# A two-layer hybrid trunk on one core: both attention heads of a tile handled as a pair, and several steps placed elsewhere in their slots

## What is computed

```python
for i in range(DEPTH):                      # 2
    h = rmsnorm(x, norm_w[i])
    (u, s5_gate, z, xbc, dt_raw, q, k, v, att_gate, merge_logits) = split(h @ w_in[i])
    y_s5 = s5_mixer(u, ...) * silu(s5_gate)            # diagonal complex SSM, gelu, GLU
    y_ssd = ssd_mixer(z, xbc, dt_raw, ...)             # dt = softplus(dt_raw + bias); 16 heads of 64
    y_att = window_attention(q, k, v, att_gate, ...)   # 16 query heads, 4 key heads, width 64
    branches = einsum('blnw,nwd->blnd', stack(y_s5, y_ssd, y_att), w_branch[i])
    x = x + (sum_n sigmoid(merge_logits)[n] * branches[n]) @ w_out[i]

# ssd_mixer, inside a chunk and across chunks: y = (C B^T * exp(segsum(a))) @ (x * dt) + x * D
# window_attention: q, k = rope(rmsnorm(.)); s = q k^T / 8, masked to two chunks
#   m = max(max(s), sink); p = exp(s - m); o = (p / (sum(p) + exp(sink - m))) @ v
```

## Time and profile before

| | us |
|---|---|
| median of 3 runs | 1928.88 (1927.85 to 1931.57) |
| the profiled execution, its own time | 1926.38 |
| its span, first to last instruction | 1924.7 |
| PE busy | 1867.9 |
| DVE busy | 1387.2 |
| ACT busy | 959.2 |

### The profile page before, as it was taken

How to read it: one execution, slowest core, us unless ns; L and a number is a source line. 1 busy time by engine, 2 the same in 40 slices (tenths; PEclk the granted TensorE clock), 3 DMA queues, 4 the chain that set the end, 5 groups by cost and what they waited for, 6 DMA issues and landing times.

```text
span 1924.7 us, 35397 instructions
## 1 busy us (share of the span) xinstructions
PE 1867.9 (97%) x11720; PEld 1574.7 (82%) x11720; DVE 1387.2 (72%) x1945; ACT 959.2 (50%) x1144; POOL 538.2 (28%) x616
## 2 busy tenths in 40 slices
PE   6999999999999999999999999999999999999998
PEld 6888888777777788888889888887777778888887
DVE  6876666777776777666678766677776876776656
ACT  5334444656656555333444344456656565543344
POOL 5053444161442010002402433442442410100043
PEclk9999999999999999999999999999999999999999
DMA  7355555556455456665554555555555555566655
GB/s 284 139 191 189 191 189 190 178 190 207 162 193 177 151 200 256 232 229 209 205 183 169 172 184 189 196 199 197 172 174 183 174 191 178 197 243 238 234 198 203
DMA packets 80785, 376.98 MB, mean 196 GB/s; under 512 B 20848, under 2 KB 27536, under 8 KB 41872
## 3 DMA queue, kind: packets, MB, share of 16 engines
q1 hardware_dynamic: 76560, 360.00, 53.5%
q0 software_dynamic: 2368, 10.99, 1.6%
q10 hardware_dynamic: 1760, 4.75, 0.6%
HBM read 356.00 MB, written 21.79 MB: 196 GB/s over the span
## 4 chain that ended last, share of the span: by engine, by line
PE 71%; DVE 10%; issue 7%; POOL 5%; ACT 3%; DMA 2%; POOLq 0%; DVEq 0%; SPq 0%; ACTq 0%
PE mm L1708 21%; PE mm L1709 10%; PE mm L1739 10%; PE mm L1741 10%; PE mm L1740 10%; DVE w_lo L1036 2%; PE mm L1692 1%; PE mm L1693 1%; PE mm L1694 1%; DMA raw<-in_stream 1%; ACT w_hi L715 1%; POOL cl L567 1%; PE b L1851 1%; POOL tB L543 1%; POOL ssum L512 1%
## 5 line engine op out<-in xcount | busy, mean ns | idle before, releaser
L1036 DVE TENSOR_TENSOR w_lo<-raw,w_hi 128x2048 fp32r<-128x2048 f32 x299 | 696.8, 2331 | 194.5 <-ACT w_hi L715 179.8
L715 ACT ACTIVATE w_hi<-raw 128x2048 fp32r<-128x2048 f32 x299 | 571.3, 1912 | 471.2 <-DMA raw<-in_stream 469.1
L1708 PE MATMUL mm<-h_both,w_hi 128*128 128x512 f32 x1792 | 635.3, 399 | 0.3 <-DVE h_both L1627 0.3
L1709 PE MATMUL mm<-h_both,w_lo 128*128 128x256 f32 x1792 | 502.4, 280 | 0.0
L1708 PEld LDWEIGHTS mm<-h_both,w_hi 128*128 128x128 f32 x1792 | 336.6, 188 | 84.5 <-DVE h_both L1627 1.0
L1709 PEld LDWEIGHTS mm<-h_both,w_lo 128*128 128x128 f32 x1792 | 338.3, 189 | 0.1
L1739 PE MATMUL mm<-w_lo,h_both 128*128 128x512 f32 x768 | 316.7, 412 | 0.0
L1741 PE MATMUL mm<-w_hi,h_both 128*128 128x512 f32 x768 | 300.6, 391 | 0.0
L1740 PE MATMUL mm<-w_hi,h_both 128*128 128x512 f32 x768 | 300.1, 391 | 0.0
L696 POOL TENSOR_TENSOR ssum<-ssum,proj 128x256 f32<-128x256 f32 x32 | 77.2, 2412 | 379.0 <-ACT proj L1005 351.9
L1739 PEld LDWEIGHTS mm<-w_lo,h_both 128*128 128x128 f32 x768 | 144.1, 188 | 41.5 <-issue 12.1
(11 more groups left out here) (338 smaller groups left out, 2674.0 us busy)
## 6 DMA issues: line engine op xcount, KB each, us to landing
raw<-in_stream SPq DMA_DIRECT2D x300, 1024.0 KB, 4.8
gscr<-gt SPq DMA_DIRECT2D x48, 256.0 KB, 6.2
gin<-gscr SPq DMA_DIRECT2D x24, 512.0 KB, 5.7
bd<-in_bdense SPq DMA_DIRECT2D x16, 384.0 KB, 5.2
lam<-lscr SPq DMA_DIRECT2D x128, 32.0 KB, 3.4
crow<-cscr POOLq DMA_DIRECT2D x16, 256.0 KB, 5.4
x_old<-out POOLq DMA_DIRECT2D x2, 2048.0 KB, 10.7
out<-proj ACTq DMA_DIRECT2D x8, 512.0 KB, 5.3
```

Of the source, the lines that this page charges most:

```text
L715: e.activation(w_hi[:, j % RAW, :], raw[:, j % RAW, :], ACT.Copy).then_inc(hi_done, 1)
L1036: e.tensor_tensor(w_lo[:, j % RAW, :], raw[:, j % RAW, :], w_hi[:, j % RAW, :].bitcast(F32), ALU.subtract).then_inc(lo_done, 1)
L1708: e.matmul(mm[:, j % 2, :], w_hi[:, j % RAW, w], h_both[:, k].rearrange("p a t -> p (a t)"), start=k == 0, stop=False)
L1709: ins = e.matmul(mm[:, j % 2, 256:512], w_lo[:, j % RAW, w], h_hi[:, k, :], start=False, stop=k == KT - 1)
```

## The change

In the gate stage the two heads of a tile are handled together. `pr`, `small` and the scores get room for both heads; `stt` and `sc` go, since the products are made in place in `ex` and `pr`. `a1`, `ssd_y`, `a2` and `a3` each issue both heads' matmuls, alternating between heads, once per tile, with scores and transposes in b7 or b5 for head 0 and b6 for head 1. `a1` and `ssd_y` stand after t3, `a2` in the fourth quarter of t5, `a3` after t5. ScalarE's `att_exp`, `att_norm` and `pt_out` and most of VectorE's steps now stand ahead of `hi` and `lo` of their slot; `back`, `scan` and `forth` of the S5 mixer too. The GELU's square stays in step 9, its tanh goes to step 10 and its last product to step 11. The sinks are negated once on GpSimd (`cur2`).

In the slices `dt_t` goes from slice 3 to 4, `dt_s` from VectorE's slot 4 to 5, `dt` from slice 5 to 6, `dt_exp` from ScalarE's slot 5 to 7, `dt_softplus` from VectorE's slot 11 to 12, `cs` from slice 13 to 15, `k_rot` from 12 to 13, `gm` from VectorE's slot 14 to 13 and the keys' rotation from 13 to 14; ScalarE's `prep_end` from 14 to 15.

```diff
@@ ScalarE, gate stage
-                        def att_exp(h):
-                            W.wait(MV, f"nm{h}")
-                            W.wait(MA, f"pn1{h ^ 1}", 0 if h else 1)
+                        def att_exp():
+                            W.wait(MV, "es")
+                            for h in range(2):
+                                for b, (lo_c, hi_c) in enumerate(((0, 128), (128, 384))):
...
                         for t in range(6):
                             s = 6 * c + t
+                            if t == 4:
+                                att_exp()
+                                att_norm()
+                            if s % QUAD == QUAD - 1:
+                                gate(s // QUAD, 0)
+                            if t == 1:
+                                inv_sqrt(MA, "q", qh[:], rq[:], rv[:], lambda: W.wait(MV, "q_v"))
+                            if t == 5:
+                                pt_out(0)
+                                pt_out(1)
+                            if s % QUAD == QUAD - 1:
+                                gate(s // QUAD, 1)
+                            if t == 1:
+                                decay_exp()
+                            hi(nb, s + LEAD)
@@ VectorE, slices
-                    if n == 11:
+                    if n == 12:
                         dt_softplus()
@@ VectorE, gate stage
-                        def st_make(h):
-                            W.wait(MA, "ex")
-                            W.wait(MP, "ys0" if h else "ys1", 0 if h else 1)
-                            MV.mark(tt_(stt_[:], ex[:, h], flat(gm[:, bass.ds(I // 2, 1), :]), ALU.mult), f"ST{h}")
+                        def st_make():
+                            W.wait(MA, "ex")
+                            MV.mark(tt_(ex[:], ex[:], gm[:, bass.ds(I // 2, 1), :].broadcast_to([P, 2, 384]), ALU.mult), "ST")
...
+                            if t == 3:
+                                att_scores()
+                                lo(nb, s + LEAD)
...
+                            if t == 4:
+                                att_sum()
...
+                                MV.mark(e.scalar_tensor_tensor(xc[:], xc[:], cc[:, 27:28], ps_ssd, ALU.mult, ALU.add), "yv")
+                                lo(nb, s + LEAD)
@@ TensorE, slices
-                    if n == 13:
+                    if n == 15:
                         W.wait(LV, "dta")
@@ TensorE, gate stage
-                        def ssd_y(h):
-                            W.wait(MV, f"ST{h}")
-                            if not h:
-                                W.wait(MV, "yatt", 1)
-                            rows = slice(64 * h, 64 * h + 64)
-                            e.matmul(ps_ssd[rows, :], xdt[:, 0, h, :], stt_[:, 0:256], start=True, stop=False)
-                            MP.mark(e.matmul(ps_ssd[rows, 128:256], xdt[:, 1, h, :], stt_[:, 256:384], start=False, stop=True), f"ys{h}")
+                        def ssd_y():
+                            W.wait(MV, "ST")
+                            for h in range(2):
+                                e.matmul(ps_ssd[64 * h:64 * h + 64, :], xdt[:, 0, h, :], ex[:, h, 0:256], start=True, stop=False)
+                            for h in range(2):
+                                ins = e.matmul(ps_ssd[64 * h:64 * h + 64, 128:256], xdt[:, 1, h, :], ex[:, h, 256:384], start=False, stop=True)
+                            MP.mark(ins, "ys")
...
+                        def a1():
...
+                            for lo_c, hi_c, q in ((0, 128, 0), (128, 384, 1)):
+                                for h in range(2):
+                                    rows = slice(64 * h, 64 * h + 64)
+                                    ins = e.matmul((b7, b6)[h][:, lo_c:hi_c], qh[rows, q * P:q * P + P], kcur[rows, 0:hi_c - lo_c], start=True, stop=True)
+                            MP.mark(ins, "A1")
...
-                                if q == 2 and t == 4:
-                                    a1(1)
                                 if q == 3 and t == 5:
-                                    a2(1)
+                                    a2()
...
                             if t == 3:
-                                ssd_y(0)
-                                a1(0)
-                            if t == 4:
-                                a2(0)
-                                ssd_y(1)
+                                a1()
+                                ssd_y()
                             if t == 5:
-                                a3(0)
-                                a3(1)
+                                a3()
```

More of the change, by code:

```diff
@@ L878, in pt_out, with att_norm @@
+                        def att_norm():
+                            W.wait(MV, "rden")
+                            for h in range(2):
+                                for b, (lo_c, hi_c) in enumerate(((0, 128), (128, 384))):
+                                    q = 28 + 2 * b + h
+                                    MA.mark(e.activation(pr[:, h, lo_c:hi_c], pr[:, h, lo_c:hi_c], ACT.Copy, scale=small[:, q:q + 1]), f"pn{b}{h}")
                         def pt_out(h):
[L879 removed]
@@ L1469, in _, with att_sum @@
+                        def att_sum():
+                            W.wait(MA, "pes")
+                            MV.mark(tt_(small[:, 24:28], small[:, 20:24], small[:, 16:20], ALU.add), "den")
+                            W.wait(MV, "den")
+                            W.wait(MA, "pn11", 1)
+                            MV.mark(e.reciprocal(small[:, 28:32], small[:, 24:28]), "rden")
                         for t in range(6):
@@ L1909, in a1 @@
-                        def a1(h):
-                            W.wait(MV, f"sc{h ^ 1}", 0 if h else 1)
-                            if not h:
-                                W.wait(MV, "qh")
-                                if c == 0:
-                                    W.wait(MG, "vcur")
-                                    e.wait_ge(k_in, keys)
-                            rows = slice(64 * h, 64 * h + 64)
-                            e.matmul(b7[:, 0:128], qh[rows, 0:P], kcur[rows, 0:P], start=True, stop=True)
-                            MP.mark(e.matmul(b7[:, 128:384], qh[rows, P:TOK], kcur[rows, :], start=True, stop=True), f"A1_{h}")
@@ new lines, in a2, with a3 @@
+                        def a2():
+                            W.wait(MA, "pn11")
+                            for h in range(2):
+                                for q in range(3):
+                                    ins = e.transpose((b5, b6)[h][:, q * P:q * P + P], pr[:, h, q * P:q * P + P], C("ident"))
+                            MP.mark(ins, "A2")
+                        def a3():
+                            W.wait(MA, "pt1")
+                            W.wait(MV, "yv")
+                            for h in range(2):
+                                e.matmul(ps_att[64 * h:64 * h + 64, :], vcur[:, 0, :], pt[:, h, 0:256], start=True, stop=False)
+                            for h in range(2):
+                                ins = e.matmul(ps_att[64 * h:64 * h + 64, 128:256], vcur[:, 1, :], pt[:, h, 256:384], start=False, stop=True)
+                            MP.mark(ins, "A3")
```

208 lines of the change are left out of this document (88 added, 120 removed).

## The result

| | before | after |
|---|---|---|
| median of the runs, us | 1928.37 (1923.67 to 1931.57) | 1878.46 (1876.60 to 1878.89) |
| the profiled execution, its own time | 1926.38 | 1878.58 |
| its span | 1924.7 | 1876.9 |
| PE busy | 1867.9 | 1826.9 |

A forecast was written before the change was run, and what follows sets the result against it. TensorE was taken as the bound (PE busy 97%). Gains of 32.0 + 6.6 + 3.4 + 4.8 + 3.2 = 50.0 us took the profiled 1926.4 to 1876.4, plus 2.5 for the median: 1878.9 us, range 1871 to 1885.

The forecast's parts named there:

- The paired matmuls: Gate stage: two stops per tile go, `a2` grows, second heads cost next to nothing; 2.00 us per tile, 32.0 us gained.
- The wait for the SSD product: Gate stage: TensorE's six waits for `stt` go, as VectorE makes the product ahead of `lo`; 6.6 us gained.
- the remaining edits: S5 steps, GELU's spread and gates: moved within slots, cost nothing as long as VectorE and ScalarE have room.
- The third rival: Gate stage: ScalarE's two-head copy before `a3` and the second gate bring small waits, about 8 us: 1887 us; chance 0.10.
- The fourth rival: Gate stage, t5: `a2` waits for both heads' probabilities, 4.5 us per tile, kernel slower at about 1950 us; chance 0.04.
- The slices: Input slices, both layers: earlier `lam_T`, shorter waits for `dta` and regained clock, 3.4 + 4.8 + 3.2 us gained.
- For `dta`: Slices: of 8.8 us of waits 4.0 come back before slice 15, 4.8 gained, plus 3.2 of lost clock.
- For `rtok`: Slices: `dt_s` leaves VectorE's slot 4, so `lam_T` comes 1.7 us earlier in both layers; 3.4 us gained.
- The offset: Whole kernel: the median of the runs lies 2.5 us above the profiled execution, 1878.9 against 1876.4 us.
- The signs named in advance: Profile after: no t4 stop, `a2` about 0.66 us, `a1` paired, no `stt` or `dta` wait, turn some 5 us shorter.

The follow-up runs named there:

- x6: The changed kernel with the second head of `ssd_y` issued alone at half of t4, and `yv` behind `lo`: 1889.4 us.
- x7: x1 with `ssd_y` issued between the two heads of `a1`, so that these are no neighbours: 1882.5 us.
- x8: The changed kernel with VectorE's remainder put back ahead of the rotated queries and the SSD product in step t2: 1891.6 us.
- x1: The changed kernel with the two steps of the GELU's inner term on VectorE moved behind the sum of the exponentials: 1872.3 us.
- x2: The changed kernel with GpSimd's last three steps on `bw` done on one column instead of 256, output not the reference's: 1862.8 us.
- x9: x1 with the two tanh for the gates on ScalarE at the end of t2 instead of t4: 1871.4 us.

## Why the prediction was right, and where it was not

The forecast was 1878.9 us, the median is 1878.5. The mechanism held, but that the number came out so close is luck: its terms erred both ways by up to 9.6 us.

- **The paired matmuls, 32.0 us: right.** The stops of 1.05 and 1.33 us went, 37.8 us; `a2` grew by 0.33 us (forecast 0.32), 5.3 us; the second head of `a1` costs 0.01 us (forecast 0.06). That is 32.5 us. The argument from the earlier trace rows, four records in the time of two, held: x6 shows it for `ssd_y` and x7 for `a1`, each by taking the heads apart. The heads of `a3` stood side by side in every run.
- **The wait for the SSD product, 6.6 us: right.** The stop after t3 fell by 6.8 us over 16 tiles. x8 shows that VectorE's order can undo it; the share of TensorE's new order is open.
- **Not counted, and gained: 5.1 us.** `a2` had waited for `pt` (3.2 us over the price of its matmuls) and `q_rot` for the queries (1.9 us). Both were small waits of before that the sum passed over; they went with the same edits.
- **The step that failed: the remaining edits at nothing.** It reasoned from VectorE's busy share of the earlier trace rows that there is room. The room was there, but not in front of the sum of the exponentials: the stops for `a3` grew by 9.6 us (9.2 us in the list of waits). The third rival had the place and nearly the price (8 us), for the wrong reason. It charged ScalarE's second copy, in every tile; the runs show 1.3 to 1.8 us in six tiles, from the GELU's inner term (x1), GpSimd's hold on VectorE (x2) and ScalarE's order (x9). In x2 the second copy is still there and the wait is not. The fourth rival's chain was estimated at 8 us from scores to transposes; `a2` never waited for it, so its margin was real. That rival divided 54 us by 16 tiles where the sum has 50.0, which is 3.1 us per tile and not 3.4.
- **The slices, 11.4 us: too small, 16.4.** For `dta` the forecast was 4.8 + 3.2 = 8.0 us. The waits of VectorE's bank reads that took its place are 3.6 us in all: 1.0 and 1.4 us before slice 15, where 1.7 and 2.3 were forecast, and 0.9 and 0.3 us before slice 13, where none was. The clock stayed at 1.00 behind those before slice 15 (windows of after, below), so 5.2 + 3.2 = 8.4 us came. For `rtok` the forecast was 3.4 us. The waits of that stop fell from 7.6 to 3.8 us, and 4.0 us of low clock behind it (3.5 by the starts, 1.4 of them luck), which I had looked for only behind `dta`, went as well; `dt_t`, now at a stop of its own, took 1.1 us back, 0.7 of them a wait for the remainder before slice 4: 6.7 us. The rest, 1.3 us, is the start of the second layer's slices.

```profile
122.60:127.00 4.40, 4.35 (x36) 4.35 (x37) 4.40 (x9) 0.83 (x2) 2.71 (x2) 1.00 0.66 242
1044.10:1048.00 3.90, 3.84 (x32) 3.85 (x33) 3.90 (x9) 0.34 (x2) 2.51 (x1) 1.00 0.63 256
```

- **The other stages, nothing: 2.8 us lost.** Of these, 1.1 us is in the eight pairs behind the gate stage (46.0 to 46.5 us in each layer), and it is there in the experiments too. The remainder lies in stages that differ by 2 us from one run of this set to another. I did not look for its cause.
- **The offset: wrong, and it hid a loss.** The forecast put the median 2.5 us above the profiled execution, as before. After the change the two are 0.1 us apart, so the profiled execution is 2.2 us over its forecast of 1876.4. In numbers: 50.0 - 4.3 (gate stage) + 5.0 (slices) - 2.8 (others) = 47.9 us gained by the profiled execution, and 1926.4 - 47.9 = 1878.5.
- **The signs named in advance**: no stop in t4, `a2` at 0.65 us, `a1` in pairs, no wait for `stt` or `dta`, waits before slice 15 at full clock (1.0 and 1.4 us, shorter than the 1.7 to 2.3 named), all came. The turn is shorter by 4.5 us instead of some 5, and a wait of `a3` for `pt` was named as the sign of the third rival.

## What to carry to other kernels

Put small matmuls that use different halves of the array next to each other: here the second head cost nothing beside the first and 1.0 us at a stop of its own. After moving work, follow the chain that each stop of the bound engine waits for, instruction by instruction on every engine in it: a busy share of 77% says nothing about what stands in front of a step of 0.15 us. And where VectorE's steps are on such a chain, look at what GpSimd does at that moment.

## What the hardware did that I had not expected

- A VectorE step of 128x4 took 1.08 us instead of 0.16, because a GpSimd instruction of 1.29 us had begun 0.23 us before it. This reached TensorE in 6 of 16 tiles: without most of that work on GpSimd (x2) the gate stages took 11.0 us less and the kernel 15.7, though GpSimd is busy for only 29% of the span.
- Issued head by head, with a matmul of the same head in between, two heads still went through together (0.93 us for eight records, 0.92 for four). With another product in between (x7) they did not.
- The clock does not follow the length of a wait alone. Behind the same wait of 2.3 us for `rtok` it was 1.00 in four executions and 0.77 to 0.79 in five (section on the slices). Behind the dearest stop for `a3` (2.84 us, with a wait of 1.73) it was 0.62; behind those of 2.77 and 2.68 us, with waits of 1.68 and 1.54, it was 1.00 (windows of after, in this order). Matmuls start up to 0.43 us apart in the first window instead of 0.23, and that is the 1.5 us by which the second layer's gate stage is longer:

```profile
1489.20:1493.50 4.30, 4.30 (x15) 3.32 (x12) 3.77 (x6) 2.66 (x4) 2.97 (x4) 0.62 0.95 336
1409.00:1413.00 4.00, 4.00 (x19) 3.27 (x18) 3.47 (x6) 2.46 (x4) 3.26 (x4) 1.00 0.95 343
407.10:411.00 3.90, 3.90 (x18) 3.19 (x19) 3.37 (x5) 2.26 (x4) 3.07 (x3) 1.00 0.95 357
```

No run here shows what decides between them.
